# Hybrid decoder step on one core: the prologue's sum of squares changes place with the last modulation tile, and each stage's first weight tile is walked by input chunk

## What is computed

```python
mod = (silu(c) @ w_ada + b_ada).reshape(rows, 9, 1, 1024)
sh1, sc1, g1, sh2, sc2, g2, sh3, sc3, g3 = mod
h = x + 0.5 * g1 * swiglu(rmsnorm(x, norm_w[0]) * (1 + sc1) + sh1, ffn_up[0], ffn_down[0])
mix_out = token_mixing(rmsnorm(h, norm_w[1]) * (1 + sc2) + sh2)   # w_in, delta rule, sparse attention, w_out
h = h + g2 * mix_out
h = h + 0.5 * g3 * swiglu(rmsnorm(h, norm_w[2]) * (1 + sc3) + sh3, ffn_up[1], ffn_down[1])
y = rmsnorm(h, final_norm_w)
```

## Time and profile before

| | us |
|---|---|
| median of 3 runs | 960.38 |
| lowest and highest | 958.53, 960.48 |
| span of the profiled execution | 961.2 |
| PE busy in it | 885.5 (92%) |
| DVE busy | 503.5 (52%) |
| ACT busy | 316.2 (33%) |

### The profile page before, as it was taken

One profiled execution on the slowest core, in us unless ns is written; L12 is line 12 of the kernel. 1 busy time (PEld: TensorE's weight loads), 2 busy tenths in 40 slices (PEclk: granted clock), 3 DMA queues, 4 the chain that ended last, 5 costly groups with the idle time before them and its releaser, 6 DMA issues.

```text
span 961.2 us, 18054 instructions
## 1 busy us (share of the span) xinstructions
PE 885.5 (92%) x6658; PEld 746.0 (78%) x6658; DVE 503.5 (52%) x978; ACT 316.2 (33%) x503; POOL 101.1 (11%) x182
## 2 busy tenths in 40 slices
PE   4689999999998999989999968899897999999996
PEld 2378898988898898876656534666777999999995
DVE  1335545445353747546666565657446555554433
ACT  1423333333323434544333611000225333333311
POOL 2000000000011000122222232330110000000011
PEclk9879999999999899999999988999998999999998
DMA  9949897877655241357768699997390555443301
GB/s 306 371 145 381 281 311 247 310 252 273 243 206 204 85 151 49 131 187 254 261 213 274 212 325 328 325 322 281 99 341 9 175 176 176 163 147 130 130 1 50
DMA packets 122464, 204.78 MB, mean 213 GB/s; under 512 B 7564, under 2 KB 56998, under 8 KB 122274
## 3 DMA queue, kind: packets, MB, share of 16 engines
q1 hardware_dynamic: 105280, 163.08, 49.6%
q0 software_dynamic: 11648, 38.45, 11.7%
q10 hardware_dynamic: 5474, 2.39, 1.0%
HBM read 199.01 MB, written 4.88 MB: 212 GB/s over the span
## 4 chain that ended last, share of the span: by engine, by line
PE 84%; DVE 6%; DMA 4%; ACT 2%; issue 2%; ACTq 1%; POOLq 0%; SPq 0%; POOL 0%; DVEq 0%
PE bank L714 18%; PE bank L715 18%; PE bank L716 18%; PE bank L678 8%; PE bank L925 3%; PE bank L1161 3%; PE bank L696 3%; PE bank L965 2%; DMA wring<-in_w_ada 2%; PE bank L744 2%; DMA kv<-in_cache_v 1%; DVE wring_rounded L1482 1%; ACTq L1410 1%; PE bank L1110 1%; DMA region<-in_state_conv 1%
## 5 line engine op out<-in xcount | busy, mean ns | idle before, releaser
L714 PE MATMUL bank<-hn_rounded,kv_rounded 128*128 128x288 f32 x928 | 281.8, 304 | 21.0 <-DVE xs_rounded L1526 10.6
L715 PE MATMUL bank<-xs_rounded,kv_rounded 128*128 128x288 f32 x928 | 277.3, 299 | 0.0
L716 PE MATMUL bank<-hn_rounded,wring_rounded 128*128 128x288 f32 x928 | 276.3, 298 | 0.0
L1482 DVE TENSOR_TENSOR wring_rounded<-wring,kv_rounded 128x1024 fp32r<-128x1024 f32 (+1 forms) x164 | 187.6, 1194 | 73.0 <-ACT kv_rounded L1222 72.9
L1222 ACT CAST kv_rounded<-wring 128x1024 fp32r<-128x1024 f32 (+1 forms) x164 | 158.7, 1027 | 162.9 <-PE bank L716 114.6
L714 PEld LDWEIGHTS bank<-hn_rounded,kv_rounded 128*128 128x128 f32 x928 | 176.8, 190 | 33.1 <-issue 13.8
L716 PEld LDWEIGHTS bank<-hn_rounded,wring_rounded 128*128 128x128 f32 x928 | 178.1, 192 | 0.0
L715 PEld LDWEIGHTS bank<-xs_rounded,kv_rounded 128*128 128x128 f32 x928 | 177.9, 192 | 0.0
L714 PE MATMUL bank<-region_rounded,kv_rounded 128*128 128x288 f32 x352 | 104.6, 297 | 0.8 <-DVE modT L1471 0.8
L715 PE MATMUL bank<-region_rounded,kv_rounded 128*128 128x288 f32 x352 | 103.8, 295 | 0.0
L716 PE MATMUL bank<-region_rounded,wring_rounded 128*128 128x288 f32 x352 | 103.5, 294 | 0.0
(11 more groups left out here) (256 smaller groups left out, 979.9 us busy)
## 6 DMA issues: line engine op xcount, KB each, us to landing
wring<-in_ffn_up SPq DMA_DIRECT2D x44, 1024.0 KB, 7.7
wring<-in_w_ada SPq DMA_DIRECT2D x36, 1024.0 KB, 10.7
wring<-in_ffn_down SPq DMA_DIRECT2D x16, 1024.0 KB, 7.3
kv<-in_cache_v SPq DMA_DIRECT2D x64, 256.0 KB, 4.7
kv<-in_cache_v POOLq DMA_DIRECT2D x64, 256.0 KB, 4.9
wring<-in_w_in SPq DMA_DIRECT2D x14, 1024.0 KB, 6.8
kv<-in_cache_k SPq DMA_DIRECT2D x44, 256.0 KB, 4.4
kv<-in_cache_k POOLq DMA_DIRECT2D x44, 256.0 KB, 4.6
```

The costliest lines, as they stand in the source:

```text
L714: nc.tensor.matmul(out, hi, rhs_hi, start=start, stop=False)
L715: nc.tensor.matmul(out, hi, rhs_lo, start=False, stop=False)
L716: return nc.tensor.matmul(out, lo, rhs_hi, start=False, stop=stop)
L1482: v.tensor_tensor(wringR[:, slot, c, :], wring[:, slot, c, :], whiR[:, u % 2, c, :], ALU.subtract).then_inc(s_wlo, 1)
```

## The change

1. SP issues `ada` tile 1 at once and then waits for the landed input x, not for the six parameter loads, before `ada` 2.
2. PE transposes the prompt right after `ada_mm(0)`; the parameters' transposes come after `ada_mm(1)`, one of them into bank 7 instead of 5. DVE copies the prompt's chunks before the parameters, and `ada_T(0)` and `ada_T(1)` wait for those copies (`s_pv`).
3. `sumsq(0)` now stands ahead of `ada_T(2)` and `ada_mm(3)`. ACT computes `rstd` (`inverse_norm(0)`) between its copies of `ada` 2 and `ada` 3.
4. The first weight tile of each of the three stages is walked chunk by chunk: for each chunk, three matmuls into each of four banks.

```diff
             load(0)
-            sp.wait_ge(s_par, 16 * 6)
-            for n in range(1, LOOP + 4):
+            load(1)
+            sp.wait_ge(s_x, 32)
+            for n in range(2, LOOP + 4):
                 load(n)
...
             def ada_T(j, odd, bank=None):
                 pe.wait_ge(s_adaev, j + 1)
+                if isinstance(j, int) and j < 2:
+                    pe.wait_ge(s_pv, j + 1)
...
+            def first_up_tile(l, slot, side):
+
+                for k in range(KD):
+                    if k % 2 == 0:
+                        pe.wait_ge(s_wlo, 4 * S1ST * l + k // 2 + 1)
+                    normed(2 * l, k)
+                    for s in range(2):
+                        for half, done in ((0, s_gate), (1, s_up)):
+                            cols = slice(256 * half + P * s, 256 * half + P * s + P)
+                            m = split_products(ps[2 * s + half][:, 0:TOK], whiR[:, side, k, cols], wringR[:, slot, k, cols],
+                                               hnR[:, k, :], xsR[:, k, :], k == 0, k == KD - 1)
+                            if k == KD - 1:
+                                m.then_inc(done, 1)
...
-            def features():
+            def param_features():
 
                 pe.wait_ge(s_par, 16 * 6)
-                T(ps[5][:, 0:105], prow[0:105, :], 105)
-                T(ps[5][:, 105:153], crow[0:48, :], 48)
+                T(ps[7][:, 0:105], prow[0:105, :], 105)
+                T(ps[7][:, 105:153], crow[0:48, :], 48)
...
             pe.wait_ge(s_cT, 1)
-            for j in range(ADA_FIRST):
-                ada_mm(j, *tile(("ada", j)))
-                if j == 0:
-                    features()
-                if j:
-                    ada_T(j - 1, (j - 1) % 2)
+            ada_mm(0, *tile(("ada", 0)))
+            prompt_features()
+            ada_mm(1, *tile(("ada", 1)))
+            param_features()
+            ada_T(0, 0)
+            ada_mm(2, *tile(("ada", 2)))
+            ada_T(1, 1)
             sumsq(0)
+            ada_T(2, 0)
+            ada_mm(3, *tile(("ada", 3)))
             ada_T(3, 1)
-            up_tile(0, 0, number[("up", 0, 0)] % RING, 0, first=True)
+            first_up_tile(0, number[("up", 0, 0)] % RING, 0)
...
             sumsq(1)
-            for turn in range(29):
+            for k in range(KD):
+                if k % 2 == 0:
+                    pe.wait_ge(s_wlo, 4 * IN0 + k // 2 + 1)
+                normed(1, k)
+                for q in range(4):
+                    cols = slice(q * P, (q + 1) * P)
+                    m = split_products(ps[q][:, 0:TOK], whiR[:, IN0 % 2, k, cols], wringR[:, number[("in", 0)] % RING, k, cols],
+                                       hnR[:, k, :], xsR[:, k, :], k == 0, k == KD - 1)
+                    if k == KD - 1:
+                        m.then_inc(s_win, 1)
+            for turn in range(4, 29):
...
             sumsq(2)
-            for j in range(3):
-                up_tile(1, j, number[("up", 1, j)] % RING, (S1ST + j) % 2, first=(j == 0))
+            first_up_tile(1, number[("up", 1, 0)] % RING, S1ST % 2)
+            for j in range(1, 3):
+                up_tile(1, j, number[("up", 1, j)] % RING, (S1ST + j) % 2)
...
+                if j == 2:
+                    inverse_norm(0)
             norm(0)
...
-            dve.wait_ge(s_pT0, 2)
-            v.tensor_copy(pvec[:, :], ps[5][:, 0:153])
-            own(v.tensor_copy(cst3[:, :, :], ps[6][:, 0:CC * 24].rearrange("p (c x) -> p c x", c=CC)))
             for c in range(KD):
                 dve.wait_ge(s_xT, c + 1)
                 v.tensor_copy(h[:, c, :], ps[c % 4][:, 0:TOK]).then_inc(s_h, 1)
+            dve.wait_ge(s_pT0, 2)
+            v.tensor_copy(cst3[:, :, :], ps[6][:, 0:CC * 24].rearrange("p (c x) -> p c x", c=CC)).then_inc(s_pv, 1)
+            v.tensor_copy(pvec[:, :], ps[7][:, 0:153]).then_inc(s_pv, 1)
+            dve.wait_ge(s_pv, 2)
```

More of the change, by code:

```diff
@@ L306, in build_program @@
         s_cT = sem("s_cT_ready")
+        s_pv = sem("s_params_copied")
         s_w = [sem(f"s_w{i}_landed") for i in range(RING)]
@@ L716, in split_products, with up_tile @@
                 return nc.tensor.matmul(out, lo, rhs_hi, start=False, stop=stop)
-            def up_tile(l, j, slot, side, first=False):
+            def first_up_tile(l, slot, side):
[10 more added lines that the diff above has]
+                                m.then_inc(done, 1)
+            def up_tile(l, j, slot, side):
                 for s in range(2):
-                    if not first:
-                        pe.wait_ge(s_hid, j * 2 + (FC * l + s - 1))
+                    pe.wait_ge(s_hid, j * 2 + (FC * l + s - 1))
                     for half, done in ((0, s_gate), (1, s_up)):
@@ L726, in up_tile @@
                                 pe.wait_ge(s_wlo, j * 4 + (4 * S1ST * l + k // 2 + 1))
-                            if first and s == 0 and half == 0:
-                                normed(2 * l, k)
                             cols = slice(256 * half + P * s, 256 * half + P * s + P)
@@ L787, in features, with prompt_features @@
                 m.then_inc(s_pT0, 1)
+            def prompt_features():
                 pe.wait_ge(s_x, 32)
@@ L830, in _ @@
                 for k in range(KD):
-                    if turn == 0:
-                        normed(1, k)
                     start, stop = k == 0, k == KD - 1
@@ L1222, in round_quarters, with inverse_norm @@
                     nc.scalar.copy(whiR[:, u % 2, c, :], wring[:, n % RING, c, :]).then_inc(s_whi, 1)
-            def norm(ni):
+            def inverse_norm(ni):
                 fn(pab[:, 3:4], eps[0:8, :], ACT.Ln)
@@ L1230, in norm @@
                 fn(rstd[:, :], rstd[:, :], ACT.Exp, scale=-0.5).then_inc(s_rstd, 1)
+            def norm(ni):
+                if ni:
+                    inverse_norm(ni)
                 if ni < 3:
```

## The result

| | before | changed |
|---|---|---|
| median, us (runs) | 960.43 (4) | 952.43 (4) |
| lowest and highest | 958.53, 964.48 | 949.96, 957.31 |
| span of the profiled execution | 961.2 | 955.7 |

The ratio is 0.991, with a 95% interval from 0.988 to 0.994: 8.0 us faster, against a forecast of 3.75. The forecast's range (951.0 to 959.8) holds the median, but the number named is 4.2 us too high; the case called quick clock gave 951.1. The profiled execution of the changed kernel is the slowest of its four timed ones (957.31).

What follows compares the result with a forecast made beforehand. PE, busy 885.5 of 961.2 us, bounds the kernel; gains come from its idle or slow time at three places. The first tile's 4.05 less 0.3 net gives 3.75, so 956.6 us, range 951.0 to 959.8.

Steps and rivals of the forecast that it cites:

- quick clock: Prologue: ada_mm(1) and all after it at the higher clock; net gain 9.25, to 951.1 us; chance 0.23.
- The bound: Whole kernel: PE busy 885.5 of 961.2 us; gain only from its idle or slow time at three places.
- Part 1, loads: Start of prologue: ada loads can be ahead by at most 1 or 2 us, worth nothing by itself.
- signs of being wrong: Gaps inside the first tile, a later ada 0 load beside ada 1, or matmul steps longer than 0.133 us.
- Part 2, prologue order: Prologue: reordered transposes, ada_mm(1) at the lower clock, clock back at 35.1, sumsq ends at 38.8.
- the late case: Prologue: clock comes back at 38.5, half of sumsq slow; gain 2.05, to 958.3 us; chance 0.25.
- Part 3, the swap: End of prologue: hides ACT's 2.28 us beside ada_mm(3); first up matmul at 48.05, 1.6 later than before.
- Part 4, the walk: First tiles: DVE never waited for again; first tile ends at 62.85, 4.05 before 66.90; w_in gains 0.3.
- The wait for `hidden`: Second FFN: next up tile waits for bank 0, 0.9 lost; net of the walk's gain, 0.3 lost.
- The sum: Whole kernel: 4.05 less 0.3 is 3.75 us gained, giving a median of 956.6 us.
- The chance of faster, 0.74: Whole kernel: faster by more than 0.2%, from all quick, nearly all forecast and half the late case.
- the forecast case: Prologue: clock comes back at 35.1, 0.45 us of sumsq slow; gain 3.75, to 956.6 us; chance 0.40.

Runs made afterwards that it cites:

- walk only: The kernel before with part 4 of the change alone, old loads and prologue kept: 955.68 us against 961.78, ratio 0.994.
- before with fill: The kernel before plus unused products on PE at the four idle places, no part of the change: 960.06 us against 962.18, ratio 0.996.
- second profile: The changed kernel profiled and timed once more, nothing altered, against the kernel before: 953.47 us against 962.55, ratio 0.991.
- the fill at one place: The changed kernel plus 12 unused products on PE between the last ada transposes and the first up tile only: 953.12 us, ratio 0.988.

## Why the prediction was right, and where it was not

**The bound** was read rightly: all the gain lies in PE's slow or idle time at the places named, and PE's busy time falls by 5.5 us only the earlier trace rows, as much as the span of the two profiled executions, since a matmul at the lower clock counts as busy for longer:

```profile
PE 880.0 (92%) x6658; PEld 744.6 (78%) x6658; DVE 503.3 (53%) x978; ACT 315.5 (33%) x503; POOL 100.7 (11%) x182
```

**Part 1, loads.** Called worth nothing. For `ada` 1 to 3 it was: each product finds its tile, and earlier loads would only have counted with the swap undone, where PE does wait for one. But one of the prediction's own signs of being wrong is there: `ada` 0 lands later. The kernel before:

```profile
14.48 3.64 PE L696 MATMUL bank<-wring,cT 128*32 128x512 f32 x16 [6.83 <-DMA wring<-in_w_ada]
```

`ada_mm(0)` starts at 14.42 to 14.48 in the three profiles with the old order of loads (before, walk only, before with fill) and at 14.73 to 15.46 in the eight with the new one, 0.5 us later on average. In the changed kernel the chain of waits up to the first `up` matmul starts with this load and has no other, so it is paid in full. That the load of `ada` 1 beside it is the reason was not tested: no run changes the loads alone.

**Part 2, prologue order: the step that failed.** The forecast had the prompt's transposes run "6 chunks at 0.54 and 2 at 0.86", with the clock falling among them as in the earlier trace rows and coming back at 35.1. It did not fall. Eight chunks took 4.3 us at 1.00, and from there the quick case came true step by step: it put `ada_mm(1)`'s end at 24.3, `ada_T(0)` at 26.3, `sumsq`'s end at 33.3, the last transposes' at 37.15, the first `up` matmul at 42.55 and the tile's end at 57.35; the rows above have 24.7, 26.7, 33.5, 37.3, 42.84 and 57.04. The argument against that case was the row 21.50 to 24.90, in which only the larger transposes ran at 0.50. But that row lies behind the fall. It tells what the clock was, not what brought it down, and the only row that bore on that was 18.05 to 21.40, which spoke for the quick case. Nor did I ask what the clock had been before: `ada_mm(0)` takes 3.6 us in every profile, so it comes up just there. The same step sank the late case, which had `ada_T(1)` break a dense stretch: at 1.00 there was nothing to set in. The Trainium skill says that the high clock did not set in for transposes (TensorE: Matmul & The Clock Gate, Part 4: PE-mode transpose); two profiles with the parameters in front agree (9.0 us of transposes, the lower rate to the end). The seven with the prompt in front show that transposes keep a clock that has come up; in four of them (4.70 to 4.93 us for 24, against 4.42) it came up 0.7 to 1.4 us into them, an estimate from these lengths and the two rates of 0.86 and 0.54 us a chunk. The 3.6 us of `ada_mm(0)` ran just ahead, and what those and the transposes each did for the rise is not told apart.

**Part 3, the swap.** Its mechanism is in the trace: `rstd` is ready at 35.95, hidden beside `ada_mm(3)`, and the chunks wait for the modulation. The forecast gave the prologue as a whole 1.6 us later; it is 3.6 earlier. Of these 3.6, undoing the swap takes 1.5 to 1.7 and undoing the new place of the parameters 3.7 to 3.9. The two don't add: in the old order PE's wait for the load of `ada` 3 takes up what the slow clock costs, and only with the swap does it count.

**Part 4, the walk.** The text reads 5.83 busy us over 46.42 to 54.10 as 24 matmuls; the row has 18, six chunks, and no later term uses the 24. Both halves of the mechanism hold: no wait for DVE in the tile, a low stretch at its start, then 0.133 us a matmul. It was sized at 62.85 − 48.05 = 14.8 us; 14.2 and 14.5 were measured, and 15.0 with the old prologue. The low stretch was taken as 4.1 us and was 2.9 in the first profile, 3.5 in the second. At `w_in` 0.3 was forecast. At turn 3's copy the changed kernel leads by 10.13 (319.62 against 329.75), at the first matmul by 9.80, with the low stretch equal in both (3.7): 0.33. The wait for `hidden` was sized at 0.9 and is 0.66; `hidden` itself takes the 1.29 us that were assumed (738.71 to 740.00). Net, 0.6 was to be lost in this tile. The next tile's first silu came 19.84 us after the first matmul in the second profile and 18.97 in the one of before (748.26 less 729.29), 0.25 of that by a low stretch longer by 0.5 us: 0.6.

**The sum.** 9.8 at `w_in`, 0.3 in it and 0.6 lost in the second FFN make 9.5; the second profile gives 9.0 by the same count, so 8.7. The timed runs say 8.0 and 9.1. The quick case had summed to 9.25. The chance of faster, 0.74, rested on the walk, which pays with either prologue; that was the sound part. That the range holds the median is owed to its lower end, which had been set at the quick case, and not to the forecast case.

**The spread.** "1 us or so" from one execution to the next was too little. The unedited stretch alone moved by 8.4 us over eleven profiles, and eight timed runs of the changed kernel lie 8.3 us apart. The 3 runs shown beforehand, 2 us apart, hid that.

**What stays open.** What about the parameters' transposes keeps or brings the clock down; and whether the fill at one place alone is worth its 1.5 us in the timed runs.

## What to carry to other kernels

When PE waits for the chunks of an input and the bank count allows it, let each chunk feed every output group of the tile: it takes DVE off the path (20.5 to 15.0 us for 96 matmuls), and with it the gaps between matmuls in which the clock stayed down or, with fill, fell again. To say what brought the clock down, read the stretch ahead of the fall; a row behind it shows only that it is down. Where an idle gap of PE ahead of dense work can't be closed, unused products in it can be worth more than they cost, but only if the work behind has no gaps of its own: at `w_in` neither the walk nor the fill alone brought more than 0.4 us, both together 2.1. And a difference in one profile is believed only where the mean clock over unedited code is the same in both.

## What the runs showed of the hardware

- Unused products in PE's idle time ahead of four stretches (5.3 to 5.5 us at three of them, 4.2 at the fourth) took 6 us off a kernel of 953 (0.986 against 0.991). The granted clock was 1.00 at the start of the first three stretches where it had been 0.50, and the 24 transposes of the fourth took 2.85 us in place of 4.50.
- Products with gaps in them, 18 matmuls busy for 5.8 of 7.7 us, did not bring the clock back, and 10 matmuls busy for 2.0 of 3.7 us, coming from 1.00, were followed by a fall. At `w_in`, with PE busy 3.43 of 4.23 us from 1.00 on, there was none.
- The same unedited code took from 411.7 to 420.0 us with the mean granted clock going from 0.98 to 0.95.
- The clock column read 1.00 in every profile over `ada_mm(0)`, which took 3.6 us where the same products take 1.92, and in two over 38 transposes that took 9.0 us in place of 5.8. Ahead of the first change that a profile shows, the durations of known instructions are the surer sign.
